# Delta-rule projection: gate sums and products placed behind earlier key pages, three query spreads at other matmul jobs, one preloaded table set

## The reference, cut to what matters

```
# delta rule, per head: conv + SiLU on q/k/v, L2 norms, gates
h = silu(causal_dwconv(x_ext, conv_w));  q, k, v = split(h)
q = q * rsqrt(sum(q*q) + 1e-6);          k = k * rsqrt(sum(k*k) + 1e-6)
beta = sigmoid(beta_in)
g = -exp(a_log) * softplus(a_in + dt_bias);   g = cumsum(g)   # per chunk
# w and q_dec use exp(g), k_dec uses exp(g_last - g)

# the 8 samples' attention over 16 cached pages of 128 keys each
s = einsum('bqhmd,bkhmd->bhmqk', q, k_pool[page_table]) * DA**-0.5 + bias
a = softmax(s)[map 1] - lam * softmax(s)[map 2];  o = a @ v_pool[page_table]
```

## Time and profile before

| | us |
|---|---|
| median of 3 runs | 2985.56 (2985.55 to 2988.97) |
| the profiled execution's own time | 2990.23 |
| its span, first to last instruction | 2988.4 |
| PE busy over the span | 2854.8 (96%), mean granted clock 0.976 |
| DVE, ACT, POOL busy | 1429.3, 890.4, 655.8 |

### The profile page before, as it was taken

The page is one execution under the profiler, slowest core; times in us unless marked ns, Lnnn a source line. Parts: engine busy times, 40 slices in busy tenths (PEclk is TensorE's granted clock), DMA queues, the critical chain, the costliest instruction groups (busy, mean ns, idle before and its releaser), DMA issues.

```text
span 2988.4 us, 42390 instructions
## 1 busy us (share of the span) xinstructions
PE 2854.8 (96%) x15556; PEld 2451.5 (82%) x15556; DVE 1429.3 (48%) x2834; ACT 890.4 (30%) x1481; POOL 655.8 (22%) x333
## 2 busy tenths in 40 slices
PE   7997687998999999999999999999999999999998
PEld 5664455667996689999999997665679999999998
DVE  3017668849894343322222235998443223333224
ACT  2016636863442221121111114444331111111113
POOL 0000003540000031122122111876012112211210
PEclk9998798999999999999999999999999999999999
DMA  3230037725553121111111101101112111111101
GB/s 108 67 129 7 0 91 218 219 81 164 155 140 123 50 68 46 42 43 55 42 42 56 42 23 41 43 29 31 43 37 63 50 42 42 56 42 42 51 26 57
DMA packets 211180, 202.20 MB, mean 68 GB/s; under 512 B 10429, under 2 KB 165650, under 8 KB 210924
## 3 DMA queue, kind: packets, MB, share of 16 engines
q1 hardware_dynamic: 195854, 184.17, 20.5%
q0 software_dynamic: 2672, 10.14, 1.2%
q10 hardware_dynamic: 12550, 6.50, 0.8%
HBM read 185.49 MB, written 17.12 MB: 68 GB/s over the span
## 4 chain that ended last, share of the span: by engine, by line
PE 67%; DVE 2%; ACT 1%; issue 0%; DMA 0%; POOL 0%; ACTq 0%; DVEq 0%
PE bank L2464 16%; PE bank L2465 16%; PE bank L2466 16%; PE bank L2788 7%; PE bank L2144 4%; PE bank L362 3%; PE bank L2773 1%; PE bank L314 1%; DVE tmp L301 0%; PE bank L2807 0%; DVE big L328 0%; PE bank L2183 0%; PE bank L2163 0%; DVE res_b L2602 0%; PE bank L2822 0%
## 5 line engine op out<-in xcount | busy, mean ns | idle before, releaser
L2464 PE MATMUL bank<-xh,wh 128*128 128x344 f32 x2112 | 675.5, 320 | 3.2 <-ACT tmp L2521 3.2
L2466 PE MATMUL bank<-xh,wl 128*128 128x344 f32 x2112 | 673.9, 319 | 0.0
L2465 PE MATMUL bank<-xl,wh 128*128 128x344 f32 x2112 | 673.5, 319 | 0.0
L2576 POOL TENSOR_TENSOR wl<-wring,wh 128x1024 fp32r<-128x1024 f32 x128 | 316.1, 2490 | 1116.1 <-ACT wh L2515 1116.1
L2594 DVE TENSOR_TENSOR tmp<-bank,tmp 128x344 f32<-128x344 f32 x132 | 68.2, 516 | 792.1 <-PE bank L2466 775.1
L2464 PEld LDWEIGHTS bank<-xh,wh 128*128 128x128 f32 x2112 | 397.4, 188 | 4.1 <-issue 3.7
L2466 PEld LDWEIGHTS bank<-xh,wl 128*128 128x128 f32 x2112 | 396.8, 188 | 0.0
L2465 PEld LDWEIGHTS bank<-xl,wh 128*128 128x128 f32 x2112 | 396.0, 188 | 0.4
L2602 DVE TENSOR_TENSOR res_b<-res_b,bank 128x344 f32<-128x344 f32 x528 | 268.2, 512 | 200.0 <-PE bank L2466 199.7
L2464 PE MATMUL bank<-hh,wh 128*128 128x344 f32 x1056 | 339.1, 321 | 0.0
L2465 PE MATMUL bank<-hl,wh 128*128 128x344 f32 x1056 | 337.9, 320 | 0.0
(11 more groups left out here) (422 smaller groups left out, 3712.7 us busy)
## 6 DMA issues: line engine op xcount, KB each, us to landing
big<-in_cache_attn_k SPq DMA_DIRECT2D x128, 256.0 KB, 3.0
big<-in_cache_attn_v SPq DMA_DIRECT2D x128, 256.0 KB, 2.9
wring<-in_ffn_w_down SPq DMA_DIRECT2D x44, 512.0 KB, 3.3
wring<-in_ffn_w_gate SPq DMA_DIRECT2D x42, 512.0 KB, 3.9
wring<-in_ffn_w_up SPq DMA_DIRECT2D x42, 512.0 KB, 3.9
wring<-in_conv_w_pw SPq DMA_DIRECT2D x24, 512.0 KB, 3.9
wring<-in_w_in SPq DMA_DIRECT2D x16, 512.0 KB, 4.7
wring<-in_w_in ACTq DMA_DIRECT2D x12, 512.0 KB, 5.0
```

Of the source, the lines that this page charges most:

```text
L2464: pe.matmul(bank_out, h, mh, start=(n == 0), stop=False)
L2465: pe.matmul(bank_out, h, ml, start=False, stop=False)
L2466: mm = pe.matmul(bank_out, l, mh, start=False, stop=(n == len(terms) - 1))
L2576: pool.tensor_tensor(wl[u][:, :], raw, wh[u][:, :].bitcast(F32), ALU.subtract).then_inc(w_cut, 1)
```

## The change

Three things are edited: where DVE's `gates_sum` and `gates_key` stand among the key pages, ahead of which jobs PE spreads the queries of samples 5, 6 and 7 (and behind which tile POOL prepares that of sample 7), and which table set ACT loads ahead of the first logarithm of each tile's norm.

```
-        QB_JOB = (1, 2, 6, 10, 14, 17, 21, 25)
+        QB_JOB = (1, 2, 6, 10, 14, 18, 22, 27)
...
             def l2_root(q):
                 i, c = q // NCH, q % NCH
+                if c == 0:
+                    act.preload_act_table_set(LN_EXP)
                 act.wait_ge(l2_mm, q + 4)
...
-                if n in (1, 3, 4, 6):
-                    query({1: 4, 3: 5, 4: 6, 6: 7}[n])
+                if n in (1, 3, 4, 5):
+                    query({1: 4, 3: 5, 4: 6, 5: 7}[n])
...
-                if p == 23:
+                if p == 14:
                     gates_sum()
-                if p == 27:
+                if p == 18:
                     gates_key()
```

## The result

| | before | changed |
|---|---|---|
| median, us | 2987.26 (4 runs) | 2970.92 (4 runs, 2969.15 to 2974.20) |
| profiled execution, own time / span | 2990.23 / 2988.4 | 2971.39 / 2969.6 |

The ratio is 0.9948, with a 95% interval of 0.9936 to 0.9960: 16 us faster. Later executions, run beside the experiments, gave 2970.86 for the changed kernel (ratio 0.9942, 0.9928 to 0.9955).

The account below looks back on a forecast made before the run. PE, busy 96%, was taken as the bound, gaining 23.9 us until DVE's key pages set the meeting at job 34: -17.8 there, +2.2 slow tail, -15.6 us in all, giving a median of 2970 us, range 2961 to 2979.

Parts of the forecast that it names:

- The first stall: PE's 15.9 us wait for ACT's logarithm ahead of a norm piece goes; PE gains 16.1 us plus 2.5 of slow tail.
- The new wait of DVE: DVE at gates_sum, now behind pair 14, waits 1.0 us for PE's sums, ready at 467.3.
- The spreads: PE's query spreads, samples 5 to 7: the 3.60 us stall and 1.8 us tail go; waits up to 1 us possible.
- The meeting: Job 34, where PE needs DVE's maxima: moves from 625.2 to 607.4, 17.8 us; PE waits there 6.1 us.
- the two additional weight loads: Two more ACT weight loads fall inside DVE's key-page run, 1.6 us each, +3.2; bounds 0 and 4.8.
- The limit of 358 GB/s: A core's HBM draw; by it additional weight loads cost key pages nothing, meeting at 604.2; speaks for rival of chance 0.24.
- The signs: In the changed profile: no ACT wait at L1161, PE waits 4 to 8 us near 607, DVE's page waits 24 us or more.
- The tail: Slow clock on PE behind its new wait at job 34, charged at 2.2 us.
- Everything after: From job 34 on, the rest of the kernel moves as one block; sum -15.6 us.
- The table set: One ACT table load of 1.28 us ahead of L1159 goes; costed at nothing.

Follow-up runs that it names:

- the run with the gates alone: The kernel before with only gates_sum and gates_key moved, behind pairs 14 and 18; query spreads and table loads as before: 2975.82 us, ratio 0.9962.
- the run with fewer table loads: The changed kernel with the preload ahead of each tile's third logarithm too, 49 table loads in place of 57: 2971.84 us, ratio 0.9948.
- The run with small loads: The changed kernel with each of twelve ACT weight tiles loaded only to its first eighth, 64 KB in place of 512 KB: 2964.62 us, ratio 0.9925.
- the one with the value pages early: The changed kernel with value pages released when DVE's last key pair is summed, not at the softmax's end: 2969.40 us, ratio 0.9947.
- The run without the table preload: The changed kernel less the table-set preload, 58 table loads on ACT in place of 57: 2971.14 us, ratio 0.9948.
- The version with the turn at job 35: The changed kernel with turn of the maxima, their spread and the sum ahead of jobs 35, 36, 39, not 34, 35, 38: 2966.63 us, ratio 0.9933.

## Why the prediction was right

**The first stall.** Forecast: fourth norm piece at 483.7, job 14 at 494.2. Measured 483.98 and 494.39, in a trace that stands 0.3 us later at that point. The new wait of DVE was 0.7 us for 1.0.

**The spreads.** No PE wait at any. Pair 31 was done at 514.8, the spread came at 516.0: 1.2 us to spare, where job 17 would have been too early; the run with the gates alone shows that wait, 3.0 us.

**The meeting.** Forecast 607.4, measured 607.4 (DVE's maxima end at 607.17 + 0.23); PE waited 5.9 us for 6.1. The mechanism was right: DVE behind its key pages is the late one, as the turn of the run with fewer table loads shows without POOL in the way. That the number is right to the tenth is luck, because two terms of the sum were wrong:
- the two additional weight loads cost less. DVE's pages ended at 602.3, at 600.8 in the kernel before. With 0.3 us of a later trace, 1.2 us for the wait that went and 0.7 us for the new one, 1.7 us are left for two loads, 0.9 each, where I took 1.6. One pair of traces says this only roughly: in the eight traces with these gates, spreads and full weight loads the pages end between +133.2 and +135.9, which makes 0 to 1.3 us a load. The run with small loads gives 0.8 to 1.0. I had put DVE's lost time down to them alone, and 12.6 us of page waits stay when the loads are small.
- the first operation on all scores took 1.6 us longer. I had this at nothing, unnamed. The two errors cancel.

This second term did more than add to the sum. The changed kernel's two traces and the one with the value pages early all have the turn at +140.24, though their key pages end at +135.1, +135.9 and +134.9. What agrees in them is POOL: its L1214 ends at +136.8 each time, L1340 (L1341 there) ends 1.1 us behind it, and the maxima follow. So the place of the meeting in these traces, 607.4, is that of a POOL operation that the forecast didn't have. Without it the pages of the first trace would have given some 605.9 (my estimate: 607.45 less the 1.58 us by which L1340 was longer), and PE would still have waited over 4 us.

The limit of 358 GB/s (the Trainium skill, "DMA: Bandwidth & Descriptors", "Specifications") as a reason for no cost at all is out: at 214 to 231 GB/s the weight loads do take page time.

**The signs.** Of those that the prediction names, one was missed: DVE's waits for key pages are 23.3 us in total, not 24 or more (24.0 in the second trace). The turn's line is L1068 in both kernels; the prediction's L1070 is a slip.

**The tail.** The job behind the new wait took 6.47 us from the turn to the next step, where 4.83 is usual: 1.6 us, forecast 2.2. At the step ahead of job 35 the changed kernel is 17.7 - 1.6 = 16.1 us ahead; the forecast had 15.6.

**Everything after.** It did not move as one block in the profile. PE's first matmul of the chunks (L1582, now L1584) is 16.1 us earlier (691.76 to 675.67), the first group of one-column matmuls (L2163, now L2165) 14.1 (930.41 to 916.30), the second one (L2183) 15.8, the start of the first FFN 17.3 (1088.87 to 1071.54), the end 18.8. Two us are given back among the chunks; 1.6 of them are here, in the changed kernel:

```profile
685.74 1.81 PE L1618 MATMUL bank<-big 128*128 128x128 f32 x8
687.35 1.91 PE L1704 MATMUL bank<-res_b,rstd 128*128 128x128 f32 x8
```

The kernel before took 1.06 us for each of the two, behind the same wait of 2.3 us for ACT; the mean granted clock of the 5 us is 1.00 there and 0.66 here. More comes again at the two one-column groups and the job behind the first, in the timeline of the changed kernel:

```profile
916.30 9.04 PE L2165 MATMUL bank<-small,big 128*128 128x1 f32 x64
925.20 6.35 PE L2146 MATMUL bank<-res_a,big 128*128 128x344 f32 x16
...
974.73 9.40 PE L2185 MATMUL bank<-small,big 128*128 128x1 f32 x64
```

And of the kernel before:

```profile
930.41 9.72 PE L2163 MATMUL bank<-small,big 128*128 128x1 f32 x64
939.99 7.33 PE L2144 MATMUL bank<-res_a,big 128*128 128x344 f32 x16
...
990.50 11.60 PE L2183 MATMUL bank<-small,big 128*128 128x1 f32 x64
```

They took 0.7, 1.0 and 2.2 us less, and nothing in the change touches them; the mean granted clock over the second group is 0.60 before and 0.75 here. From the first group to the first FFN the kernel before takes 158.5 us and the changed kernel 155.2 (155.1 in its second trace). The run without the table preload takes 160.1, though its program is the same there: it comes to the first group 4.8 us ahead of the changed kernel and loses all of it. So of the 18.8 us between the two profiled executions some 3 belong to how these stretches fell, and 1.6 went the other way in the chunks. The medians moved by 16.3 us, near the 16.1 of job 35 and the 15.6 of the forecast; with several us decided by the clock behind the stage, a part of that agreement is luck too. Why the clock falls in one execution's stretch and not in the other's was not tried.

**The table set** did what the order of instructions says, one load less. It spares PE 0.8 us by job 14, in time that PE has to spare at the turn, and was worth nothing that can be measured in the total.

The version with the turn at job 35 is the faster one by medians, about 4 us under the changed kernel, though the intervals overlap. It takes away the wait that the change had put at job 34.

## What to carry to other kernels

A wait that is handed through three engines (DVE late with a small copy, ACT behind it, PE behind ACT) is removed by moving the small copy to one pair behind its cause. But before the gain is summed on the engine that stood still, find the next place where it meets another engine, and work out when that one arrives; here 5.9 of 23.9 us were lost at that meeting, and a constant that fixes its place (which job the turn precedes) had to be moved with the change to get some 4 us of the wait and its tail back. When one engine gets faster, count what it issues beside the others' streams.

## What the runs showed of the hardware

A DVE operation on two SBUF tensors (128x1024 f32) takes 1.22 us alone. In all twelve traces it took that if no POOL tensor operation was under way at its start, and otherwise ended 1.07 to 1.09 us behind the end of POOL's: in the second trace of the changed kernel 601.26 + 2.00 = 603.26 for POOL and 602.37 + 1.97 = 604.34 for DVE; 604.02 and 605.09 in the first. The cost is 0.2 to 1.7 us, by how long POOL's operation still has to go. The rule is in the Trainium skill, "SBUF — State Buffer", section "Who interferes with whom": of a DVE instruction with two SBUF inputs and a GpSimd one that reads SBUF, the one that comes second waits until the first has ended. The traces agree, the other way round too: in the kernel before DVE's L1338 was first, and POOL's L1212, begun at 601.50 inside it, took 2.77 us for the usual 2.36. The page operations (L1260) have one input in PSUM and kept 1.22 us beside POOL.

A wait of PE of 5.9 us cost 1.6 us of slow clock, one of 5.2 us (fewer table loads) 2.0 us, one of 3.0 us (gates alone) 1.8 us, and one of 3.6 us the 1.8 us of the earlier trace rows. But one of 3.5 us at the turn (without the table preload) cost nothing, with the granted clock at 1.00 over the 6 us behind it, and the wait of 2.3 us in the chunks was followed by 1.6 us of it in the changed kernel and by none in the kernel before. So the length of a wait alone doesn't say whether the clock falls behind it.
